# One raw weight buffer exchanged for one more rounded one, and roundings placed three units ahead instead of two

## The reference, cut to what matters

```
h = rms_norm(x);  u = h @ w_in                      # iq ik dk kc vc ks kw dq nq xbc sz mg
ya, yb, yc = sparse attention, block-sparse attention, state-space mixer (conv, scan, rms_norm)
mix = g0*(ya @ br_dsa) + g1*(yb @ br_nsa) + g2*(yc @ br_ssd);  x = x + mix @ w_out
h = rms_norm(x);  x = x + square(relu(h @ ff1)) @ ff2
# second block, layer 0 ("even")
p = rms_norm(h) @ w_in_even;  u = val * sigmoid(glu)
ya = silu(layernorm(causal conv of 31 taps(u))) * silu(a_gate)
yb = (pooled differences of b_val @ pool_w) * silu(b_gate);  h = h + [ya, yb] @ w_out_even
# layer 1 ("odd")
xr, gate = rms_norm(h) @ w_in_odd;  xc = conv(xr)
y = linear recurrence from xc and two sigmoids of (xc @ w_rg, xc @ w_ig);  h = h + (y * silu(gate)) @ w_out_odd
return rms_norm(h)
```

## Time and profile before

| what | us |
|---|---|
| median of 3 runs (lowest to highest) | 1131.89 (1131.25 to 1133.16) |
| the profiled execution | 1133.29 |
| its span, first to last instruction | 1131.5 |
| TensorE busy (matmul) | 1068.9 (94%) |
| TensorE busy (weight load) | 1005.1 (89%) |
| VectorE busy | 728.3 (64%) |
| GpSimd busy | 600.9 (53%) |
| ScalarE busy | 591.6 (52%) |
| DMA, mean over the span | 140 GB/s |

### The profile page before, as it was taken

The page is one execution under the profiler, slowest core; times in us unless marked ns, Lnnn a source line. Parts: engine busy times, 40 slices in busy tenths (PEclk is TensorE's granted clock), DMA queues, the critical chain, the costliest instruction groups (busy, mean ns, idle before and its releaser), DMA issues. The chain is left out here.

```text
span 1131.5 us, 21394 instructions
## 1 busy us (share of the span) xinstructions
PE 1068.9 (94%) x8189; PEld 1005.1 (89%) x8189; DVE 728.3 (64%) x1498; ACT 591.6 (52%) x1178; POOL 600.9 (53%) x453
## 2 busy tenths in 40 slices
PE   8899999999999989999999999999988988998986
PEld 8699888998889979989999999999978877998976
DVE  7849576666653334784575543327999877597864
ACT  5345657766664466754455554334333426477631
POOL 3537344445454467645534444448686655576751
PEclk9989999999999989999999999999999988998988
DMA  8324333333234433235545555554544433543432
GB/s 298 107 78 150 112 113 112 110 115 112 95 104 140 141 102 113 75 114 185 181 163 181 184 187 183 172 179 158 169 148 150 131 112 100 208 140 112 168 113 75
DMA packets 43157, 158.08 MB, mean 140 GB/s; under 512 B 4912, under 2 KB 4912, under 8 KB 42672
## 3 DMA queue, kind: packets, MB, share of 16 engines
q1 hardware_dynamic: 42912, 156.69, 41.4%
q10 hardware_dynamic: 144, 0.03, 0.0%
HBM read 155.65 MB, written 1.05 MB: 138 GB/s over the span
## 5 line engine op out<-in xcount | busy, mean ns | idle before, releaser
L1747 PE MATMUL p_proj<-arena_r,ring_hi 128*128 128x256 f32 x2208 | 663.6, 301 | 24.0 <-POOL ring_lo L554 12.0
L1748 PE MATMUL p_proj<-arena_r,ring_hi 128*128 128x256 f32 x2208 | 631.5, 286 | 0.0
L1749 PE MATMUL p_proj<-arena_r,ring_lo 128*128 128x256 f32 x2208 | 631.2, 286 | 0.0
L554 POOL TENSOR_TENSOR ring_lo<-ring,ring_hi 128x1024 fp32r<-128x1024 f32 x182 | 438.4, 2410 | 320.1 <-ACT ring_hi L886 319.1
L1747 PEld LDWEIGHTS p_proj<-arena_r,ring_hi 128*128 128x128 f32 x2208 | 430.0, 195 | 42.2 <-issue 24.0
L1748 PEld LDWEIGHTS p_proj<-arena_r,ring_hi 128*128 128x128 f32 x2208 | 430.6, 195 | 8.2 <-issue 6.0
L1749 PEld LDWEIGHTS p_proj<-arena_r,ring_lo 128*128 128x128 f32 x2208 | 430.1, 195 | 0.0
L886 ACT ACTIVATE ring_hi<-ring 128x1024 fp32r<-128x1024 f32 x276 | 290.5, 1053 | 119.7 <-PE p_proj L1749 118.4
L554 DVE TENSOR_TENSOR ring_lo<-ring,ring_hi 128x1024 fp32r<-128x1024 f32 x94 | 116.3, 1238 | 70.0 <-ACT ring_hi L886 68.8
L662 POOL TENSOR_TENSOR sbuf_s<-sbuf_s,srow 128x256 f32<-128x256 f32 (+1 forms) x48 | 42.8, 892 | 83.5 <-DVE srow L1311 58.9
L909 ACT ACTIVATE arena_r<-arena 128x256 fp32r<-128x256 f32 x108 | 42.6, 408 | 48.2 <-DVE arena L1476 22.3
(11 more groups left out here) (272 smaller groups left out, 1232.9 us busy)
## 6 DMA issues: line engine op xcount, KB each, us to landing
ring<-w_stream SPq DMA_DIRECT2D x286, 512.0 KB, 3.3
arena<-w_tok SPq DMA_DIRECT2D x1, 1632.0 KB, 12.8
arena<-w_rgi SPq DMA_DIRECT2D x1, 1536.0 KB, 8.2
arena<-x_t SPq DMA_DIRECT2D x4, 256.0 KB, 5.5
arena<-w_cmp SPq DMA_DIRECT2D x1, 1024.0 KB, 14.8
out_t<-arena SPq DMA_DIRECT2D x4, 256.0 KB, 2.4
par<-cols SPq DMA_DIRECT2D x1, 323.0 KB, 3.2
row<-rows ACTq DMA_DIRECT2D x1, 32.0 KB, 3.4
```

Of the source, the lines that this page charges most:

```text
L554: return eng.tensor_tensor(ring_lo[:, u % RING, :, :].rearrange("p k n -> p (k n)"), ring[:, u % RING, :, :].rearrange("p k n -> p (k n)") ...
L1747: pe.matmul(slot(s)[:, 0:S], w_hi, hi, start=(c == 0), stop=False)
L1748: pe.matmul(slot(s)[:, 0:S], w_hi, lo, start=False, stop=False)
L1749: mm = pe.matmul(slot(s)[:, 0:S], w_lo, hi, start=False, stop=(c == n - 1))
```

## The change: what it does

Three constants change. There are four raw buffers in place of five and four rounded buffers in place of three, so the memory of both together stays the same. The load of unit u now waits until TensorE is through with unit u - 4. The step `wsplit` of unit u stands ahead of the job that starts at unit u - 3. The loads of `w_tok` and `w_cmp` are issued ahead of unit 4 instead of unit 5. No instruction is added or removed, and no stream of weights is changed.

```diff
--- before.py
+++ after.py
@@ -25,9 +25,9 @@
 LRU_H = 12
 CONV_K = 31
 WINDOWS = (2, 4, 8, 16)
-RING = 5
-HIS = 3
-AHEAD = 2
+RING = 4
+HIS = 4
+AHEAD = 3
 TOK = 408
 TOK_IW, TOK_NG, TOK_DT, TOK_DV, TOK_VS, TOK_VW = 0, 8, 56, 88, 152, 280
```

## The result

| | before | after |
|---|---|---|
| median of the runs, us | 1131.57 (4 runs) | 1165.14 (4 runs, 1161.71 to 1173.92) |
| ratio, 95% interval | | 1.031 [1.024, 1.037] |
| the profiled execution, its span | 1133.29, 1131.5 | 1161.71, 1160.0 |
| TensorE busy (8189 matmuls) | 1068.9 | 1073.9 |
| VectorE busy | 728.3 | 777.0 |

The kernel became 33.6 us slower by the medians, 28.5 by the spans of the two profiled executions (the profiled one of the changed kernel is the fastest of its four). I had forecast 14.1. Of the 28.5, 5.0 are TensorE's own busy time for the same matmuls (mean granted clock 0.964 against 0.968), and 23.5 are idle time of TensorE.

The account below looks back on a forecast made before the run. TensorE's pace bounds the kernel nearly everywhere, with chains through VectorE and ScalarE at stage seams. Seams and gates sum to +10.7 us, with clock +14.1, giving a median of 1146.0; forecast's own range 1136 to 1156, 8 in 10 1131 to 1159.

Parts of the forecast that it names:

- lnout: Layer norm's end: unit 242's late rounding stands ahead of ScalarE's chain that TensorE waits for; +3.2 us, bounds +1.5 and +4.
- the gates: Gate jobs: unit 264's rounding moves ahead of nine square roots, ending a 3.72 us stop; net -3.6, bounds -6 and 0.
- w_out 0: Seam br_ssd to w_out: unit 122's remainder ahead of VectorE's multiply delays block 7; +2.6 us, bounds 0 and 3.3.
- the price of a stop in clock: New stops of 2.6 and 2.9 us at w_out 0 and w_rgi: 1.7 us each, +3.4, bounds 0 and +6.8.
- Three PSUM slots cover this in mid-stage: Mid-stage: job u-3's reading, 1.5 us later on ScalarE, 2.7 on VectorE, is covered by the slots.
- Start: Kernel start: units 4 and 6 rounded ahead of iq 0's scaling and ik's copies; +2.3 us, bounds 0 and +4.1.
- w_out and ff1: Seams into w_out (+2.6) and ff1 (+1.3, unit 130 ahead of w_out 7's add), with 1.7 us of clock.
- w_rgi: Unit 247's load, behind w_rgi, goes out one unit later and reaches TensorE late; +2.9 us, bounds 0 and +4.
- Val_glu to a_gate: From ff2: convolution +2.9, vanished remainder stops worth 1.79, a_gate 0 +0.9; sum +2.0 us, bounds -1.8 and +3.8.
- (a): Rival, whole kernel faster: seam delays are covered and removed stops count in full; about 1124 us, chance 0.12.
- (b): Rival, whole kernel unchanged: gate gain and seam costs cancel; 1132 us, chance 0.11.
- (c): Rival, worse: TensorE waits for loads in steady stretches, landings 5.0 us instead of 3.3; about 1160 us, chance 0.10.

Follow-up runs that it names:

- e2: Kernel before, with only the roundings and remainders placed three units ahead instead of two (five raw, three rounded buffers); 1150.41 us, ratio 1.017.
- e9: Against the kernel before: five raw and four rounded buffers, roundings three ahead (two to unit 23), remainders two ahead; 1123.51 us, ratio 0.9935.
- e3: Changed kernel with five raw buffers instead of four (four rounded, roundings and remainders three ahead); 1137.71 us, ratio to the kernel before 1.006.
- e8: As e3, five raw and four rounded buffers, roundings three ahead, but all remainders two ahead; 1127.33 us, ratio to the kernel before 0.995.
- e15: Kernel before, with two chained one-input copies on GpSimd in place of each weight remainder, leaving those units without a true remainder; 1109.96 us.
- e13: Kernel before, with a single one-input copy on GpSimd in place of each weight remainder, leaving those units without a true remainder; 1092.79 us.

## Why the prediction was wrong

**Right, by its own steps.** The unit mechanism (load released at the end of u-4, landing 3.3 us later, ScalarE and VectorE late for job u-3); steady stretches at no cost (0.0 us over ff1 and ff2); lnout (load of unit 242 from 961.36, landed 964.58; the chain began 4.2 us after unit 238 instead of 1.1, and TensorE lost 3.4 to unit 242, predicted 3.2); the gates (no stop before unit 264, the roots behind its rounding, -3.9 at that unit and -2.7 over the stretch, predicted -3.6); w_out 0 (a stop of 3.34 us before block 7, predicted 2.6); the first convolution step (4.9 us after the end of unit 195 instead of 2.2, so +2.7, predicted 2.9); the price of a stop in clock (behind the one at w_out 0 the granted clock was 0.50 for 3.4 us). That the clock's total came near (+5.0 of TensorE's busy time, predicted 3.4) is partly luck: other stretches at 0.50 are new at xbc 2, xbc 6 and xbc 17, where I had no stop.

**The step that failed.** "Three PSUM slots cover this in mid-stage (the slot is wanted 5.8 us later)." I applied this to everything in those lists, and so gave units 24 to 101, a third of the time, no term. They cost 13.8 us. In them all three helpers also serve the attention heads and the mixer, whose steps are wanted at once: the copy L841 (a stop of 1.61 us) and the scaling L671 (0.99) are two. Nor did the slots themselves hold: xbc 2 and xbc 6 began as soon as VectorE had read their slot, after stops of 3.67 and 2.01 us. And I had no term for GpSimd's own list, nor for what its remainders do to VectorE when they fall elsewhere: L1287 took 2.4 us for 0.4 at both of these, and the eight L562 at br_dsa 0 took 9.70 us for 5.80, with TensorE waiting 6.65 behind them (2.76 before). All of my seams were places where the next stage begins; the attention is a seam at each of its steps. How the 13.8 us divide between late loads and held-up instructions is open: the raw buffer takes back 12.4 of them, the copies on GpSimd 6.1.

**Sizes.** Start: 6.9 for 2.3, and not for the reason given. I had w_cmp behind a load; e2, with the old order of loads, lost the same (7.6). What stood there is unit 2's remainder ahead of the first squares, which began at 16.09 instead of 13.29, and further roundings and remainders ahead of the head jobs' scaling; e9, with two ahead for the roundings and remainders there, lost none of it. w_out and ff1: 9.4 for 5.6; ff1's seam alone cost 3.8 us (units 122 to 129) for 1.3, by the way that I had, but the load of unit 130 took 4.9 us where I had 3.3. w_rgi: the load landed in 7.2 us, not 9.1, and unit 247 was not what TensorE waited for; but ScalarE stood 4.82 us before it, the copy L907 and VectorE's chain behind, and TensorE 3.73 us for the square at its end. In that chain L1110 took 2.23 us beside a GpSimd remainder. The step at unit 246 was 4.3 us, predicted 2.9 and 1.7 of clock: a price that came near by another way, which is luck. The Trainium skill's fixed part and rate (DMA: Bandwidth & Descriptors, Anatomy of one DMA) gave an estimated 6.8 us for it. The section has them for DMAs that GpSimd issues, and these go from SyncE; this run's 7.2 lies near, the 9.1 of before does not. Val_glu to a_gate: -4.3 for +2.0. The convolution began late as predicted, but I had carried that through to the mean, and VectorE caught up: for the same 280 instructions from the first step to the mean it was busy 118.6 us instead of 125.7, and TensorE waited 0.25 us for it there instead of 3.31. I had priced when VectorE starts and what it waits for, not how long its instructions are held up, and this gain was luck.

**Rivals.** (a) and (b) needed covered seams and fell. (c) had the size (1160) but not the cause: landings in the changed kernel have the median of 3.3 us as before, not 5.0, though single ones at seams took 4.9 and 5.2. The range ended at 1159 because I took the sum of named seams for all of them.

## What to carry to other kernels

Before moving a step ahead in an in-order list, ask of each thing behind it when it is wanted, in every stage that the list serves, and not only of the loop that the step belongs to. Rounding further ahead pays only if load and destination are both free by then: the two buffers rise together, and one taken from the other turns 5 us of short ring into 33. Even with both the whole order three ahead still lost 6 us (e3); it paid once the remainders stayed two ahead (e8, e9). And a gain from taking an engine's work away proves nothing about a change until the same is done to the kernel before.

## What the runs showed of the hardware

VectorE stands still when it starts an instruction with two inputs in SBUF while GpSimd runs a subtraction from SBUF; it ends 0.3 us after GpSimd's over 128x256, and 0.02 us after it over 128x2. Timelines of the changed kernel, VectorE and GpSimd, twice:

```profile
597.89 2.25 DVE L1110 SCALAR_TENSOR_TENSOR arena_r<-arena,par,arena_r 128x256 fp32r<-128x256 f32 x1 [0.33 <-ACT arena_r L907]
...
597.46 2.39 POOL L554 TENSOR_TENSOR ring_lo<-ring,ring_hi 128x1024 fp32r<-128x1024 f32 x1 [4.25 <-ACT ring_hi L886]
...
271.74 2.28 DVE L1311 TENSOR_TENSOR srow<-srow,gates 128x2 f32<-128x2 f32 x1
...
271.65 2.35 POOL L554 TENSOR_TENSOR ring_lo<-ring,ring_hi 128x1024 fp32r<-128x1024 f32 x1 [3.34 <-ACT ring_hi L886]
```

Alone L1110 takes 0.48 us, and L1311, over two elements, 0.16. Instructions with one of their two inputs in PSUM are not touched: L1117 takes 0.43 in all of its seven meetings with GpSimd. An output there does not help: L1442, from two inputs in SBUF to PSUM, takes 1.94 us at 1075.37 beside such a subtraction, and 0.43 alone. The Trainium skill says so (SBUF — State Buffer, "Who interferes with whom": "A DVE instruction with two SBUF inputs contends with a GpSimd instruction that reads SBUF", by an exclusive lock, and one with at most one SBUF input does not), and these rows agree. What I had not expected is its worth in both kernels: 21 us with two copies of 1.05 us in place of the remainder (e15) and 39 with one (e13). How much of that is the shorter hold-up and how much GpSimd's own shorter time isn't separated.
